# A mixture-of-experts kernel: small experts take three products with 64 columns in gate and up, and keep the joined operand in the down projection

## The reference

```
logits = h @ w_router                      # 256 x 8
top_v, top_i = top_k(logits, 2);  top_w = softmax(top_v)
gates[t, e] = top_w where e is one of the token's two experts, else 0
y = sum over e of gates[:, e] * ((silu(h @ w_gate[e]) * (h @ w_up[e])) @ w_down[e])
```

## Time and profile before

| | |
|---|---|
| time, median of 3 runs | 1433.79 us (1429.02 to 1434.1) |
| the profiled execution's own time | 1420.63 us |
| its span, first to last instruction | 1418.8 us |
| mean granted TensorE clock | 0.986 of full |
| PE, DVE, ACT busy | 96%, 77%, 66% of the span |
| moved by DMA | 439.13 MB, mean 310 GB/s |

### The profile page before, as it was taken

The page is one execution under the profiler, slowest core; times in us unless marked ns, Lnnn a source line. Parts: engine busy times, 40 slices in busy tenths (PEclk is TensorE's granted clock), DMA queues, the critical chain, the costliest instruction groups (busy, mean ns, idle before and its releaser), DMA issues.

```text
span 1418.8 us, 16608 instructions
## 1 busy us (share of the span) xinstructions
PE 1369.0 (96%) x6550; PEld 1143.2 (81%) x6550; DVE 1097.6 (77%) x871; ACT 940.6 (66%) x767; POOL 49.3 (3%) x51
## 2 busy tenths in 40 slices
PE   8999999999999999999999999999999999999887
PEld 7886788887988788877888878878887878888766
DVE  4786644556465988888898898798898889888796
ACT  3565534335455677777777788687777777777764
POOL 0000000000010000000000000000000000002000
PEclk9999999999999999999999999999999999999998
DMA  9744455555632899999999999999999989999993
GB/s 311 214 159 149 155 205 178 178 179 177 224 119 92 334 373 382 379 387 399 322 407 390 364 400 407 393 366 398 379 374 414 408 324 397 394 368 392 412 360 115
DMA packets 136643, 439.13 MB, mean 310 GB/s; under 512 B 11520, under 2 KB 28912, under 8 KB 120816
## 3 DMA queue, kind: packets, MB, share of 16 engines
q1 hardware_dynamic: 130688, 424.24, 80.0%
q0 software_dynamic: 3392, 12.07, 2.5%
q10 hardware_dynamic: 2480, 1.69, 0.4%
HBM read 432.20 MB, written 5.78 MB: 309 GB/s over the span
## 4 chain that ended last, share of the span: by engine, by line
PE 73%; DVE 17%; ACT 5%; DMA 3%; issue 3%; ACTq 0%; SPq 0%; DVEq 0%
PE ps L2003 18%; PE ps L2005 18%; PE ps L2004 18%; DVE lo L1286 12%; PE ps L2575 7%; PE ps L2495 4%; PE ps L2496 4%; ACT hi L790 2%; DMA raw<-in_od_w_gate_dram 2%; PE ps L2560 1%; DMA wr<-in_od_w_router_dram 1%; ACT work L1098 1%; DVE work L1312 0%; PE ps L2299 0%; DMA x<-in_x_dram 0%
## 5 line engine op out<-in xcount | busy, mean ns | idle before, releaser
L1286 DVE TENSOR_TENSOR lo<-raw,hi 128x2048 fp32r<-128x2048 f32 (+1 forms) x403 | 904.9, 2285 | 102.9 <-ACT hi L790 101.2
L790 ACT ACTIVATE hi<-raw 128x2048 fp32r<-128x2048 f32 (+1 forms) x403 | 766.8, 1914 | 206.4 <-PE ps L2005 157.0
L2003 PE MATMUL ps<-hi,xT_hi 128*128 128x512 f32 (+1 forms) x752 | 294.6, 392 | 7.2 <-DVE lo L1286 4.6
L2005 PE MATMUL ps<-hi,xT_lo 128*128 128x512 f32 (+1 forms) x752 | 290.0, 386 | 0.0
L2004 PE MATMUL ps<-lo,xT_hi 128*128 128x512 f32 (+1 forms) x752 | 289.7, 385 | 0.0
L2495 PE MATMUL ps<-hi,xT_hi 128*128 128x512 f32 x448 | 187.4, 418 | 12.0 <-DVE lo L1286 11.0
L2496 PE MATMUL ps<-lo,xT_hi 128*128 128x512 f32 x448 | 181.4, 405 | 0.0
L2003 PEld LDWEIGHTS ps<-hi,xT_hi 128*128 128x128 f32 x752 | 141.7, 188 | 38.3 <-issue 5.5
L2005 PEld LDWEIGHTS ps<-hi,xT_lo 128*128 128x128 f32 x752 | 141.4, 188 | 28.7
L2004 PEld LDWEIGHTS ps<-lo,xT_hi 128*128 128x128 f32 x752 | 141.6, 188 | 26.4
L2495 PEld LDWEIGHTS ps<-hi,xT_hi 128*128 128x128 f32 x448 | 88.5, 198 | 45.5 <-DVE lo L1286 19.9
(11 more groups left out here) (327 smaller groups left out, 1223.9 us busy)
## 6 DMA issues: line engine op xcount, KB each, us to landing
raw<-in_od_w_gate_dram SPq DMA_DIRECT2D x112, 1024.0 KB, 8.4
raw<-in_od_w_up_dram SPq DMA_DIRECT2D x112, 1024.0 KB, 9.4
raw<-in_od_w_down_dram SPq DMA_DIRECT2D x112, 1024.0 KB, 8.3
raw<-in_od_w_qkv_dram SPq DMA_DIRECT2D x12, 1024.0 KB, 5.2
raw<-in_ev_w_gate_dram SPq DMA_DIRECT2D x11, 1024.0 KB, 5.2
raw<-in_ev_w_up_dram SPq DMA_DIRECT2D x11, 1024.0 KB, 5.1
raw<-in_ev_w_down_dram SPq DMA_DIRECT2D x11, 1024.0 KB, 5.1
raw<-in_ev_w_in_dram SPq DMA_DIRECT2D x4, 1024.0 KB, 11.1
```

The lines of the kernel that those rows point to most:

```text
L790: act.activation(unit(hi, n), unit(raw, n), ACT.Copy).then_inc(hi_ready, 1)
L1286: dve.tensor_tensor(unit(lo, n), unit(raw, n), unit(hi, n).bitcast(F32), ALU.subtract)\
L2003: pe.matmul(out, s_hi, m_hi, start=start, stop=False, skip_group_check=True)
L2005: return pe.matmul(out, s_lo, m_hi, start=False, stop=stop, skip_group_check=True)
```

## The change

For small experts the gate and up products go the way of the large ones, with 64 columns in place of 128: `three` with `xg_hi[:, k, 0:64]` and `xg_lo[:, k, 0:64]`, then silu and multiply on 64 rows, and a plain transposition of 64 rows by 128 columns with the 64 x 64 identity. The transposed block (128 x 256) is split straight out of PSUM into the two halves of the joined operand, and the down projection goes on as before with `both`. `turn`, `fold64`, `keep_gate`, `keep_up`, the four `turned_` steps, their buffers and semaphores go, and so do the lists of steps of their own that small experts had on ACT, DVE and PE: all experts now run through the list of the large ones. The core of the diff:

```diff
+        def rows_of(e):
+
+            return HALF if e in SMALL else P
...
-                        if e in SMALL:
-                            ins = both(ps[:, bank + m, :], xg_hi[:, k, :], wh[:, kk, cols], wl[:, kk, cols], k == 0,
-                                       k == KD - 1)
-                            continue
-                        ins = three(ps[:, bank + m, :], xg_hi[:, k, :], xg_lo[:, k, :], wh[:, kk, cols],
-                                    wl[:, kk, cols], k == 0, k == KD - 1)
+                        ins = three(ps[0:tokens, bank + m, :], xg_hi[:, k, 0:tokens], xg_lo[:, k, 0:tokens],
+                                    wh[:, kk, cols], wl[:, kk, cols], k == 0, k == KD - 1)
...
-                act.activation(work[:, 0, 0:w], ps[:, 4:4 + w // W, :].rearrange("p a n -> p (a n)"), ACT.Silu)\
+                n = rows_of(e)
+                act.activation(work[0:n, 0, 0:w], ps[0:n, 4:4 + w // W, :].rearrange("p a n -> p (a n)"), ACT.Silu)\
                     .then_inc(g_silu_done, 1)
...
+                n = rows_of(e)
+                dve.tensor_tensor(work[0:n, 1, 0:w], work[0:n, 0, 0:w],
+                                  ps[0:n, 2:2 + w // W, :].rearrange("p a n -> p (a n)"), ALU.mult).then_inc(g_h_done, 1)
...
+                n = rows_of(e)
                 for j in range(4):
-                    ins = pe.transpose(ps[:, 7, P * j:P * j + P], work[:, 1, f + j:f + W:4], ident[:])
+                    ins = pe.transpose(ps[:, 7, n * j:n * j + n], work[0:n, 1, f + j:f + W:4], ident[0:n, 0:n])
                 ins.then_inc(g_hT_done, 1)
...
+                if e in SMALL:
+                    act.activation(hT_both(s)[:, :, 0:HALF], ps[:, 7, 0:SEQ].rearrange("p (j q) -> p j q", q=HALF),
+                                   ACT.Copy).then_inc(g_hT_hi_ready, 1)
+                    return
...
+                if e in SMALL:
+                    dve.tensor_tensor(hT_both(s)[:, :, HALF:P], ps[:, 7, 0:SEQ].rearrange("p (j q) -> p j q", q=HALF),
+                                      hT_both(s)[:, :, 0:HALF].bitcast(F32), ALU.subtract).then_inc(g_hT_ready, 1)
+                    return
```

More of the change, by code:

```diff
@@ L384, in build @@
         y_out = work[:, 3, :]
-        swish, h_turned = (probT[:, t].rearrange("p h q -> p (h q)").rearrange("p (s n) -> p s n", s=2) for t in range(T))
         results = nc.alloc_sbuf_tensor_at("results", [P, 2 * T, D], F32, offset=arena_at)
@@ L1066, in gathered_high @@
                     act.wait_ge(gathered, 2 * e + b + 1)
-                    if e in SMALL:
-                        act.activation(xg_hi[:, 4 * b:4 * b + 4, 0:HALF], ps[:, 4 + b, 0:SEQ].rearrange(
-                            "p (k s) -> p k s", k=4), ACT.Copy).then_inc(xg_hi_ready, 1)
-                        continue
-                    act.activation(xg_hi[:, 4 * b:4 * b + 4, :], ps[:, 4 + b, :].rearrange("p (k s) -> p k s", k=4),
-                                   ACT.Copy).then_inc(xg_hi_ready, 1)
+                    n = rows_of(e)
+                    act.activation(xg_hi[:, 4 * b:4 * b + 4, 0:n], ps[:, 4 + b, 0:4 * n].rearrange(
+                        "p (k s) -> p k s", k=4), ACT.Copy).then_inc(xg_hi_ready, 1)
             def y_copy(e):
@@ L1148, in _ @@
                         y_copy(e - 1)
[L1149 to L1198, removed]
                     used(UP_AT[0])
@@ L1849, in _ @@
                         used(0)
-                    if e in SMALL:
-                        used(GATE_AT[1] + 2)
-                        turned_multiply(e, 0)
-                        used(GATE_AT[1] + 3)
-                        turned_low(e, 0)
-                        used(UP_AT[1])
-                        if e == 1:
-                            slot_numbers()
-                        used(GATE_AT[2])
-                        if e + 1 < NE:
-                            make_place(e + 1)
-                        used(GATE_AT[2] + 2)
-                        turned_multiply(e, 1)
-                        used(GATE_AT[2] + 3)
-                        turned_low(e, 1)
-                        used(UP_AT[2])
-                        turned_multiply(e, 2)
-                        used(UP_AT[2] + 1)
-                        turned_low(e, 2)
-                        if e + 1 < NE:
-                            pick(e + 1)
-                        used(DOWN_AT[1])
-                        if e == NE - 1:
-                            for i in range(2 * T):
-                                used(DOWN_AT[1] + i + 1)
-                                add_result(i)
-                        used(GATE_AT[3] + 2)
-                        turned_multiply(e, 3)
-                        used(GATE_AT[3] + 3)
-                        turned_low(e, 3)
-                        used(UP_AT[3])
-                        turned_multiply(e, 4)
-                        used(UP_AT[3] + 1)
-                        turned_low(e, 4)
-                        used(DOWN_AT[2] + 1)
-                        turned_multiply(e, 5)
-                        used(DOWN_AT[2] + 2)
-                        turned_low(e, 5)
-                        used(DOWN_AT[2] + 3)
-                        turned_multiply(e, 6)
-                        used(DOWN_AT[3])
-                        if e + 1 < NE:
-                            gathered_low(e + 1)
-                        turned_low(e, 6)
-                        continue
                     used(GATE_AT[1])
@@ L2452, in gather @@
             def gather(e):
-                if e in SMALL:
-                    pe.wait_ge(rows_landed, 16 * e)
-                    pe.wait_ge(g_silu_done, NCH * e)
-                    for k in range(KD):
-                        ins = pe.transpose(ps[:, 4 + k // 4, HALF * (k % 4):HALF * (k % 4) + HALF], rows[0:HALF, P * k:P * k + P],
-                                           ident[0:HALF, 0:HALF])
-                        if k % 4 == 3:
-                            ins.then_inc(gathered, 1)
-                    return
                 if e:
@@ L2465, in gather @@
                     pe.wait_ge(g_silu_done, NCH * e)
+                    n = rows_of(e)
                     for k in range(KD):
-                        ins = pe.transpose(ps[:, 4 + k // 4, P * (k % 4):P * (k % 4) + P], rows[:, P * k:P * k + P], ident[:])
+                        ins = pe.transpose(ps[:, 4 + k // 4, n * (k % 4):n * (k % 4) + n], rows[0:n, P * k:P * k + P],
+                                           ident[0:n, 0:n])
                         if k % 4 == 3:
@@ L2500, in columns @@
                 n = first_of(e) + base + q
+                tokens = rows_of(e)
                 w = MOE_CHUNKS[c][1]
@@ L2558, in g_transpose_h @@
                 f = W * (s - SUBS[c][0])
+                n = rows_of(e)
                 for j in range(4):
-                    ins = pe.transpose(ps[:, 7, P * j:P * j + P], work[:, 1, f + j:f + W:4], ident[:])
-                ins.then_inc(g_hT_done, 1)
-            def turn(e, s, c):
-                pe.wait_ge(g_silu_done, NCH * e + c + 1)
-                pe.wait_ge(g_h_done, NCH * e + c + 1)
-                if s:
-                    pe.wait_ge(t_h_done, small_subs(e, s))
-                else:
-                    pe.wait_ge(g_hT_ready, NSUB * e)
-                f = W * (s - SUBS[c][0])
-                for part in range(2):
-                    for j in range(4):
-                        first = SEQ * part + HALF * j
-                        ins = pe.matmul(ps[:, 7, first:first + HALF], work[:, part, f + j:f + W:4], fold64[:],
-                                        start=True, stop=True)
+                    ins = pe.transpose(ps[:, 7, n * j:n * j + n], work[0:n, 1, f + j:f + W:4], ident[0:n, 0:n])
                 ins.then_inc(g_hT_done, 1)
@@ L2605, in _ @@
                     gate(e, 1, 0, 1)
-                    if e in SMALL:
-                        if e == SMALL[0]:
-                            pe.wait_ge(order_ready, 1)
-                        turn(e, 0, 0)
-                        gate(e, 1, 2, 3)
-                        up(e, 1, 0, 1, 2, 3)
-                        pe.wait_ge(y_copied, e)
-                        down(e, 0, 0, 1)
-                        if e == NE - 1:
-                            transpose_place(e)
-                        gate(e, 2, 0, 1)
-                        turn(e, 1, 1)
-                        gate(e, 2, 2, 3)
-                        turn(e, 2, 1)
-                        if e + 1 < NE:
-                            pick_rows(e + 1)
-                        up(e, 2, 0, 1, 2, 3)
-                        down(e, 1, 0, 1, 2, 3)
-                        gate(e, 3, 0, 1)
-                        turn(e, 3, 2)
-                        gate(e, 3, 2, 3)
-                        turn(e, 4, 2)
-                        up(e, 3, 0, 1, 2, 3)
-                        down(e, 2, 0)
-                        turn(e, 5, 3)
-                        down(e, 2, 1, 2)
-                        turn(e, 6, 3)
-                        down(e, 2, 3)
```

(4 more changed lines are left out.)

42 lines of the change are left out of this document (2 added, 40 removed).

## The result

The changed kernel takes 1409.03 us (median of 4 runs, 1406.88 to 1410.67), the kernel before 1431.4 (median of 4 runs, 1424.79 to 1434.1). The ratio is 0.985, 95% interval 0.981 to 0.989. Forecast were 1413 us and 0.9855 of the median.

A forecast was written before the change was run, and what follows sets the result against it. Small experts were held by folds, the lower clock they bring and DVE's queue, afterwards by PE. Three at 110.4 us plus 112.9 make 444.1 against 465.2; 21 us off the median 1433.79 gives 1413, range 1402 to 1434.

The forecast's parts named there:

- PE's own work, +3.5 us an expert: Small experts: more gate and up matmuls and transpositions, no folds; PE's sum 106.4 us an expert, 3.5 more than before.
- the 6% that narrow operands might have given: Gate and up matmuls with 64 stationary columns: up to 6% shorter step, 4.6 us an expert, kept only as low end.
- The clock, -12.8 us: Small experts: 64 matmuls slowed to 0.43 us behind folds return to full clock, 12.8 us off, at most 16.
- Waits: PE late for DVE's splits, mainly in down units: with restarts 4.0 us in experts 1, 3 and 5.
- the end of an expert: Chunk 3's down: DVE's last splits come late by 2.5 us; the next expert can start at t = 18.9.
- DVE 98.5 us, idle about 12: Small expert: DVE's work goes from 97.1 to 98.5 us, below PE's 106.4, with about 12 us idle.
- Expert lengths: Experts 1, 3 and 5 at 110.4 us, expert 7 at 112.9; sum 444.1 against 465.2, 21 us less.
- DMA: Weight transfers in small experts: 104.6 us at 421 GB/s or 111.8 at 394; no cost taken.
- The first rival: DMA takes over: three small experts at 394 GB/s, 111.8 us, 113.8 with late splits; 1426 us in all, chance 0.12.
- Rivals 2, 3, 4: Small experts: clock still falls (1426, chance 0.08); DVE's queue stays the bound (1457, 0.12); 64 columns lower the clock (1682, 0.03).
- the point of 17.8 us: DVE idle time in a small expert from which DVE's queue decides, at 116.3 us an expert.
- the third rival: DVE's queue stays the bound: 98.5 us plus idle time, 120.8 an expert, 1457 in all, chance 0.12.

The follow-up runs named there:

- the fourth experiment: Changed kernel with eight fold matmuls put back ahead of each of a small expert's seven transpositions: 1534.61 us, ratio 1.074 to the kernel before.
- the first: The kernel before, unchanged, run again for a second profile: median 1428.95 us of 10 runs, profiled span 1428.7 us.
- the third: Kernel before with its eight fold matmuls replaced by eight plain 64-row transpositions, result incomplete: 1387.01 us, ratio 0.970.
- the second experiment: Changed kernel without the low x high product of gate and up in small experts, result incomplete: 1382.97 us, ratio 0.969 to the kernel before.

## Why the prediction was right

The time (1409 against 1413), the sign and the mechanism came out: the folds went, the clock came back, and PE's own work now sets the small experts' length. That the time is within 4 us is in part luck, as the line on the experts' lengths says. Term by term, for the four small experts:

- *PE's own work, +3.5 us an expert:* measured +5.4 (21.6 / 4). Mis-sized were the 64-row transpositions, taken as 0.39 us by the row for 128 rows, measured 0.62 (+1.6 an expert; the 0.10 ahead of them, 0.6 to 0.7 an expert, stand in the row of the waits), and the step of a matmul, 0.2295 in small experts against the 0.227 of the large one (+0.3 on 112 of them). The small experts of the kernel before had 0.2295 too, so that is not due to 64 columns. Of the 6% that narrow operands might have given, nothing came.
- *The clock, -12.8 us:* 68 slow matmuls to none, -13.6. Right, and by the fourth experiment due to the folds; by the first and the third not to them alone.
- *Waits:* 41.4 to 18.7, where the forecast left 4.0 for each of three experts and 6.6 for expert 7, 18.6 with restarts of the down stages. That the two agree to 0.1 is chance, since the 18.7 hold 2.4 us of the break and all restarts. Without restarts the forecast had 15.8 for late splits, and 14.2 with the restarts behind them were measured. In time the end of an expert came out to 0.2 us (18.7 for 18.9).
- *DVE 98.5 us, idle about 12:* 99.1 and 13.1 in expert 3. *ACT* 90.8 to 87.0.
- *Expert lengths:* 112.0 to 112.8 for 110.4, 113.6 for 112.9. The sum was 6 us short for these four: it took 21 us off and the two profiles differ by 14.7. The medians hid this, because the profiled execution from which I took 465.2 was faster than most (471.7 in the second), and this error nearly cancels that of the sum.
- *DMA:* nothing taken, and nothing came: 390 GB/s, with 410 to be had. The first rival's 111.8 us was too slow a bound, since 394 GB/s in the earlier trace rows was the demand and not the limit; the second experiment gives 106.6.
- *Rivals 2, 3, 4:* the clock is 1.00 with 64 columns and with 64-row transpositions at this density, and DVE's idle time fell under the point of 17.8 us (11.1 to 13.4 in the four experts). The idle time now, which the third rival took as 15.4 to 17.9 us, is that of experts 1, 3 and 5; in expert 7 the rows have 21.1.

The rule of the Trainium skill on a drain at a change of tiling mode (TensorEngine Tiling, Key Properties), left out of the sum because the rows for 16 columns spoke against it, fits what the 64 rows do: 0.1 us into them and some 0.2 back. In this case the number of columns did not bring it on: passing from 64 to 128 stationary columns, the next matmul starts after 0.23 us as elsewhere. The number of rows did; that it is such a drain is argued, not shown.

## What to carry to other kernels

A trick that saves matmuls must be charged with what it puts between the engines: two products instead of three saved PE 25.7 us an expert (112 matmuls of 0.2295), the fold that they needed took 24.7 back, its 3.5 us pieces brought the clock down, and DVE, which works its list in order, stood still behind each of the seven (13.0 us in expert 3). Before a unit of work is moved into an engine's spare time, the spare time is to be compared stage by stage and unit by unit, not in sum. And a transfer rate in a profile is a limit only where somebody waits for it.

## What the runs showed of the hardware that I had not expected

Four plain transpositions of 64 rows by 128 columns in a stream of 128-row matmuls cost 0.72 us of PE's time, of 128 rows 0.40 us. Matmuls with 64 stationary columns run at the same step as with 128 (0.2295 us with 512 moving columns), though their weight load takes 0.13 us in place of 0.19. Two executions of one kernel had 68 and 83 matmuls at the lower clock in the small experts, at different places, and the second lost another 3 us to it ahead of them.
